# Attention's up product and the output product of a mixer as three fp32r passes over split operands, on one Trainium2 core

## The reference, cut to what matters

```python
y_attn = dsa_branch(q, k, v, qi, ki, wi)                  # 256 x 512
merged = (sigmoid(g_ssm) * (y_ssm @ w_ssm_up)
          + sigmoid(g_attn) * (y_attn @ w_attn_up))       # w_attn_up: 512 x 1024
h = h + merged @ w_out                                    # w_out: 1024 x 1024
hn = rmsnorm(h, norm2_g)
h = h + peer_ffn(hn, peer_wq, ...)                        # starts with hn @ peer_wq
```

## Time and profile before

| what | value |
|---|---|
| median of 3 runs | 2242.0 us (2241.77 to 2243.59) |
| time of the profiled execution | 2244.5 us |
| its span | 2242.8 us, mean granted TensorE clock 0.968 |
| PE busy | 2077.7 us (93%) |
| PEld | 1720.3 us (77%) |
| DVE | 1610.0 us (72%) |
| ACT | 1131.2 us (50%) |
| POOL | 693.7 us (31%) |

### The profile page before, as it was taken

The page is one execution under the profiler, slowest core; times in us unless marked ns, Lnnn a source line. Parts: engine busy times, 40 slices in busy tenths (PEclk is TensorE's granted clock), DMA queues, the critical chain, the costliest instruction groups (busy, mean ns, idle before and its releaser), DMA issues. The chain is left out here.

```text
span 2242.8 us, 33580 instructions
## 1 busy us (share of the span) xinstructions
PE 2077.7 (93%) x11164; PEld 1720.3 (77%) x11164; DVE 1610.0 (72%) x2587; ACT 1131.2 (50%) x1641; POOL 693.7 (31%) x468
## 2 busy tenths in 40 slices
PE   5898999996999889999888999899899999999998
PEld 4775767775877776777676656899899999888887
DVE  4367888887367888888878651399779998555555
ACT  5352767774335376777550233355444444445454
POOL 6620040001757504000030004599967773000000
PEclk8997999998999989999989999999999999999999
DMA  9864789995457658899832333255444445555554
GB/s 394 310 219 148 298 305 354 343 347 193 178 201 294 246 189 322 339 347 343 306 100 75 111 109 146 88 174 174 163 136 145 141 140 180 193 188 191 191 189 150
DMA packets 76634, 485.70 MB, mean 217 GB/s; under 512 B 9472, under 2 KB 9984, under 8 KB 58624
## 3 DMA queue, kind: packets, MB, share of 16 engines
q1 hardware_dynamic: 75824, 482.88, 59.2%
q10 hardware_dynamic: 720, 1.61, 0.2%
HBM read 483.41 MB, written 1.05 MB: 216 GB/s over the span
## 5 line engine op out<-in xcount | busy, mean ns | idle before, releaser
L1191 DVE TENSOR_TENSOR moe_w_lo<-ring,moe_w_hi 128x1024 fp32r<-128x1024 f32 x384 | 467.1, 1252 | 52.1 <-ACT moe_w_hi L1115 38.3
L1115 ACT ACTIVATE moe_w_hi<-ring 128x1024 fp32r<-128x1024 f32 x376 | 385.1, 1058 | 75.0 <-PE bank L1048 43.2
L3083 POOL TENSOR_TENSOR peer_u_lo<-peer_u,peer_u_hi 128x512 fp32r<-128x512 f32 x253 | 343.3, 1368 | 97.0 <-ACT peer_u_hi L3108 95.0
L3023 PE MATMUL bank<-peer_hn_hi,peer_u_hi 128*128 128x256 f32 x1024 | 295.7, 289 | 17.9 <-POOL peer_u_lo L3083 11.9
L3024 PE MATMUL bank<-peer_hn_lo,peer_u_hi 128*128 128x256 f32 x1024 | 287.6, 281 | 0.0
L3025 PE MATMUL bank<-peer_hn_hi,peer_u_lo 128*128 128x256 f32 x1024 | 287.4, 281 | 0.0
L229 POOL TENSOR_TENSOR ret_all_w_lo<-ring,ret_all_w_hi 128x1024 fp32r<-128x1024 f32 x64 | 158.1, 2479 | 293.7 <-ACT ret_all_w_hi L219 293.1
L3108 ACT ACTIVATE peer_u_hi<-peer_u 128x512 fp32r<-128x512 f32 x253 | 159.2, 629 | 129.7 <-PE bank L3025 120.4
L1029 PE MATMUL bank<-moe_w_hi,moe_slots_hi 128*128 128x512 f32 x512 | 210.5, 411 | 11.7 <-DVE moe_w_lo L1191 7.7
L3023 PEld LDWEIGHTS bank<-peer_hn_hi,peer_u_hi 128*128 128x128 f32 x1024 | 194.7, 190 | 19.9 <-POOL peer_u_lo L3083 13.6
L1031 PE MATMUL bank<-moe_w_hi,moe_slots_lo 128*128 128x512 f32 x512 | 201.0, 393 | 0.0
(11 more groups left out here) (517 smaller groups left out, 4570.4 us busy)
## 6 DMA issues: line engine op xcount, KB each, us to landing
ring<-in_stream SPq DMA_DIRECT2D x135, 2048.0 KB, 8.3
peer_u<-in_peer_u SPq DMA_DIRECT2D x128, 512.0 KB, 3.2
peer_scores<-in_peer_v SPq DMA_DIRECT2D x86, 512.0 KB, 4.3
sb_mod_ring<-in_ada_t SPq DMA_DIRECT2D x64, 512.0 KB, 6.4
peer_u<-in_peer_v SPq DMA_DIRECT2D x42, 512.0 KB, 4.3
ret_mod_ring<-in_ada_t SPq DMA_DIRECT2D x32, 512.0 KB, 5.0
s_bz<-in_b_channel SPq DMA_DIRECT2D x4, 512.0 KB, 5.8
ring<-in_stream SPq DMA_DIRECT2D x2, 1024.0 KB, 5.0
```

Of the source, the lines that this page charges most:

```text
L1115: act.activation(w_hi[:, q, :], K.ring[:, at % RING, q * CHUNK // Q:(q + 1) * CHUNK // Q], ACT.Copy).then_inc(hi_done, 1)
L1191: dve.tensor_tensor(w_lo[:, q, :], K.ring[:, at % RING, q * CHUNK // Q:(q + 1) * CHUNK // Q], w_hi[:, q, :].bitcast(F32), ALU.subtract).th ...
L3023: pe.matmul(out, u_hi[:, b, k2, :], h_hi[:, k, :], start=(k == 0), stop=False)
L3083: pool.tensor_tensor(u_lo[:, b, :, :], u[:, i, KD // 2 * half:KD // 2 * (half + 1), :], u_hi[:, b, :, :].bitcast(F32), ALU.subtract).then_ ...
```

## The change

The products of `attn_up` and `project_out` become three fp32r passes each. The 12 quarters of the three weight chunks are rounded on ACT (`split_high`) into rooms that are free then: `queries.w_hi` for attn_up, `queries.w_lo` for n_out, a new `out_w_hi` for n_out+1. GpSimd writes the low parts in place over the ring (`ring_low` is the ring's own memory, read as fp32r). ACT and DVE split the attention output (`attended_high`, `attended_low`) and the merged block (`mixed_hi`, `mixed_low`). A new wait, `act.wait_ge(K.chunk_used, n_out + 1)`, stands ahead of `queries.high`.

```diff
@@ -289,6 +289,8 @@
     sb = lambda n, shape, dt=F32: scope.enter_context(K.nc.sbuf_tensor(n, shape, dt))
     K.hT = sb("hT", [P, KD, T])
     K.mod = sb("mod", [P, 3 * D])
+    with ExitStack() as same_place:
+        K.ring_low = same_place.enter_context(K.nc.sbuf_tensor("ring_low", [P, RING, CHUNK], F32R))
     K.ring = sb("ring", [P, RING, CHUNK])
     K.c_row = sb("c_row", [P, D])
     K.mods, K.mod_bias = sb("mods", [P, 4, MODS]), sb("mod_bias", [P, 4, MODS])
@@ -1935,6 +1937,8 @@
         self.K = K
         NT = S5_TILES
         sb = lambda n, s, scope=scope: scope.enter_context(K.nc.sbuf_tensor(n, s, F32))
+        with ExitStack() as later:
+            self.mixed_hi, self.mixed_lo = (later.enter_context(K.nc.sbuf_tensor(f"mixed_{n}", [P, KD, T], F32R)) for n in ("hi", "lo"))
         self.uT = sb("uT", [P, 4, T])
         self.qT = sb("qT", [P, 4, T])
         self.qiT = sb("qiT", [P, 2, T])
@@ -1957,6 +1961,8 @@
         self.rope = K.c_row[:].rearrange("p (a b t) -> p a b t", a=2, b=2)
     def more_tables(self, scope):
+        with ExitStack() as later:
+            self.high_room = later.enter_context(self.K.nc.sbuf_tensor("out_w_hi", [P, CHUNK], F32R))
         self.last_tables = scope.enter_context(self.K.nc.sbuf_tensor("s5_tables_b", [P, S5_TILES * T], F32))
     def load(self, sp):
@@ -1999,7 +2005,12 @@
         s_(s) for s in ("idx_made", "relu", "score", "score_masked", "pick", "pick_masked"))
     l_made, l_used, max_ready, exp_done, p_ready, p_turned, pT_ready, o_made, o_copied = (
         s_(s) for s in ("l_made", "l_used", "max", "exp", "p", "p_turned", "pT", "o_made", "o_copied"))
-    attn_made, m_ready, m_turned, m_taken = (s_(s) for s in ("attn_made", "m", "m_turned", "m_taken"))
+    attn_made, m_ready, m_turned, m_high, m_low = (s_(s) for s in ("attn_made", "m", "m_turned", "m_high", "m_low"))
+    up_high, up_low, ya_high, ya_low = (s_(s) for s in ("up_high", "up_low", "ya_high", "ya_low"))
+    UP = (n_attn, n_out, n_out + 1)
+    up_rooms = [w[:].rearrange("p q c -> p (q c)") for w in (queries.w_hi, queries.w_lo)] + [S.high_room[:]]
+    quarter = lambda q: slice(q * CHUNK // 4, (q + 1) * CHUNK // 4)
+    ya_halves = [x[:, 0:4, :] for x in (queries.x_hi, queries.x_lo)]
     out_made, x_added, squared, half_ready, std_made, norm_in, hn_ready, hn_turned, hn_high = (
         s_(s) for s in ("out_made", "x_added", "squared", "half_ready", "std", "norm_in", "hn", "hn_turned", "hn_high"))
     hn = K.mod[:, 0:2 * D].rearrange("p (t d) -> p t d", t=TT)
@@ -2069,6 +2080,11 @@
                 pool.wait_ge(pick_ready, tt + 1)
                 pool.affine_select(out=bias[:, tt, own(tt)], in_=bias[:, tt, own(tt)], compare_op=ALU.is_ge, fill=NEG, base=0,
                                    pattern=[[-1, P]], channel_multiplier=1).then_inc(pick_masked, 1)
+            for i, n in enumerate(UP):
+                for q in range(4):
+                    pool.wait_ge(up_high, 4 * i + q + 1)
+                    pool.tensor_tensor(K.ring_low[:, n % RING, quarter(q)], K.ring[:, n % RING, quarter(q)],
+                                       up_rooms[i][:, quarter(q)].bitcast(F32), ALU.subtract).then_inc(up_low, 1)
             queries.low(pool, queries.n0, True)
         @block.tensor
@@ -2278,13 +2294,19 @@
             def attn_up(tt, dh):
-                if tt == 0 and dh == 0:
-                    wait_chunk(pe, K, n_attn)
-                pe.wait_ge(o_copied, 4 * tt + 4)
+                pe.wait_ge(ya_low, tt + 1)
                 pe.wait_ge(pT_ready, len(units))
                 if tt == 1:
                     pe.wait_ge(ssm_taken, 3 + dh)
-                upward(n_attn, S.yaT, tt, dh, 4 + 2 * tt + dh).then_inc(K.chunk_used if tt and dh else attn_made, 1)
+                high, low = (w.rearrange("p (k c) -> p k c", k=4) for w in (up_rooms[0], K.ring_low[:, n_attn % RING, :]))
+                cols, out = slice(dh * 512, (dh + 1) * 512), K.bank[:, 4 + 2 * tt + dh, :]
+                for k in range(4):
+                    pe.wait_ge(up_low, k + 1)
+                    x_high, x_low = (x[:, k, own(tt)] for x in ya_halves)
+                    pe.matmul(out, x_high, high[:, k, cols], start=(k == 0), stop=False)
+                    pe.matmul(out, x_high, low[:, k, cols], start=False, stop=False)
+                    last = pe.matmul(out, x_low, high[:, k, cols], start=False, stop=(k == 3))
+                last.then_inc(K.chunk_used if tt and dh else attn_made, 1)
             def turn_mixed(tt):
                 for half in range(2):
@@ -2296,13 +2318,16 @@
             def project_out(tt, dh):
-                if tt == 0:
-                    wait_chunk(pe, K, n_out + dh)
-                pe.wait_ge(m_taken, 2 * tt + 2)
+                pe.wait_ge(m_low, 2 * tt + 2)
                 pe.wait_ge(l_used if tt else o_copied, len(units))
-                w = K.ring[:, (n_out + dh) % RING, :].rearrange("p (k c) -> p k c", k=KD)
+                high, low = (w.rearrange("p (k c) -> p k c", k=KD) for w in (up_rooms[1 + dh], K.ring_low[:, (n_out + dh) % RING, :]))
+                out = K.bank[:, 2 * tt + dh, :]
                 for k in range(KD):
-                    last = pe.matmul(K.bank[:, 2 * tt + dh, :], K.hT[:, k, own(tt)], w[:, k, :], start=(k == 0), stop=(k == KD - 1))
+                    pe.wait_ge(up_low, 4 * (1 + dh) + (k // 2 + 1))
+                    x_high, x_low = (x[:, k, own(tt)] for x in (S.mixed_hi, S.mixed_lo))
+                    pe.matmul(out, x_high, high[:, k, :], start=(k == 0), stop=False)
+                    pe.matmul(out, x_high, low[:, k, :], start=False, stop=False)
+                    last = pe.matmul(out, x_low, high[:, k, :], start=False, stop=(k == KD - 1))
                 last.then_inc(K.chunk_used if tt == 1 else out_made, 1)
             def turn_normed(tt):
@@ -2449,6 +2474,16 @@
                                K.bank[:, 4 + n % 2, 0:2 * (tt + 1) * P].rearrange("p (m t) -> p m t", t=P),
                                ACT.Copy).then_inc(pT_ready, 1)
+            def split_high(i, q):
+                n = UP[i]
+                if q == 0:
+                    act.wait_ge(K.landed[n % RING], 16 * (n // RING + 1))
+                act.activation(up_rooms[i][:, quarter(q)], K.ring[:, n % RING, quarter(q)], ACT.Copy).then_inc(up_high, 1)
+
+            def attended_high(tt):
+                act.wait_ge(o_copied, 4 * tt + 4)
+                act.activation(ya_halves[0][:, :, own(tt)], S.yaT[:, :, own(tt)], ACT.Copy).then_inc(ya_high, 1)
+
             exponentials(0)
             for n in range(len(units)):
                 if n + 1 < len(units):
@@ -2456,13 +2491,21 @@
                 take_turned(n)
                 if n < TT:
                     take_gate(8 + n, n_last, 3, ACT.Copy)
+                if n >= 4:
+                    for q in (2 * (n % 2), 2 * (n % 2) + 1):
+                        split_high(n // 2 - 2, q)
+                if n == 6:
+                    attended_high(0)
             act.wait_ge(group_taken, 10)
             act.activation(gates[:, 1, :, COLS:D], gates[:, 1, :, COLS:D], ACT.Sigmoid).then_inc(gates_open, 1)
+            attended_high(1)
+            for q in range(4):
+                split_high(2, q)
             for tt in range(TT):
                 for half in range(2):
                     act.wait_ge(m_turned, 2 * tt + half + 1)
-                    act.activation(K.hT[:, 4 * half:4 * half + 4, own(tt)],
-                                   K.bank[:, 4 + 2 * tt + half, :].rearrange("p (k t) -> p k t", k=4), ACT.Copy).then_inc(m_taken, 1)
+                    act.activation(S.mixed_hi[:, 4 * half:4 * half + 4, own(tt)],
+                                   K.bank[:, 4 + 2 * tt + half, :].rearrange("p (k t) -> p k t", k=4), ACT.Copy).then_inc(m_high, 1)
             def square(n):
@@ -2485,6 +2528,7 @@
                 act.activation(queries.x_hi[:, 4 * half:4 * half + 4, own(tt)],
                                K.bank[:, 4 + n, :].rearrange("p (k t) -> p k t", k=4), ACT.Copy).then_inc(hn_high, 1)
+            act.wait_ge(K.chunk_used, n_out + 1)
             queries.high(act, queries.n0, True)
             square(0)
             square(1)
@@ -2695,6 +2739,17 @@
                 dve.tensor_tensor(gates[:, 0, tt, cols], gates[:, 0, tt, cols], K.bank[:, 6 + g % 2, :],
                                   ALU.mult).then_inc(ssm_taken, 1)
+            def attended_low(tt):
+                dve.wait_ge(ya_high, tt + 1)
+                high, low = (x[:, :, own(tt)] for x in ya_halves)
+                dve.tensor_tensor(low, S.yaT[:, :, own(tt)], high.bitcast(F32), ALU.subtract).then_inc(ya_low, 1)
+
+            def mixed_low(n):
+                tt, ks = n // 2, slice(n % 2 * 4, n % 2 * 4 + 4)
+                dve.wait_ge(m_high, n + 1)
+                dve.tensor_tensor(S.mixed_lo[:, ks, own(tt)], K.bank[:, 4 + n, :].rearrange("p (k t) -> p k t", k=4),
```

(10 more changed lines are left out.)

## The result

The change makes the kernel slower by 0.65%: 2258.9 us median (2254.6 to 2260.5, four runs) against 2242.8 us (2241.8 to 2245.1, four runs), ratio 1.0065 (95% interval 1.0054 to 1.0077). Slower was forecast; 2250.0 was not, and 2258.9 lies beyond the range's upper end of 2254.5. A second set of five runs of the same kernel gave 2258.8 us, ratio 1.0062 (1.0048 to 1.0076).

What follows compares the result with a forecast made beforehand. It took TensorE's own work to bound the mixer's end until 1372, then a 6.26 us latency chain. +6.2 to project_out and later delays summed to +8.3, taken as +8: 2252.5 profiled, 2250.0 median, range 2244.5 to 2254.5.

Steps and rivals of the forecast that it cites:

- the sign: Whole kernel: slower, 2250.0 us for the median (+0.36%); chance of slower by over 0.2% put at 0.75.
- the mechanism: Mixer's end: a VectorE instruction with two SBUF operands ends no sooner than 0.54 us after the GpSimd subtraction it meets.
- The late high parts: After project_out(1,0): ACT's peer_wq high parts start only then, take 3.78 us and put square(0) at 1371.2.
- such ones are free: VectorE beside GpSimd: one-operand instructions lose nothing, judged from L2737, which took 0.15 us.
- divide(5): VectorE's divide in unit 5: meets a subtraction, ends at 1319.0, +0.9 us, hidden but for 0.1 behind TensorE.
- the first rival: No mutual blocking; its 3.9 us idle before turn(7) may cost the clock, half speed for 3 us costing 1.5; chance 0.20.
- the forecast's own line: Last turn and attn_up: divide(7) ends at 1332.5, turn(7) is 5.5 us late, attn_up starts about 1335.3 instead of 1329.4.
- +6.2 to project_out: First project_out: starts at 1350.2 against 1344.01, +6.2 us, with TensorE's 2.7 us saving in attn_up inside.
- blocked twice: Sums, lows and divide(7): GpSimd goes first, each may lose another 2.3 us; +12 to +13, 2254.5 us; chance 0.13.
- L1754's worst is 2.61 us, one subtraction: Retention stage's VectorE instruction, at worst 2.61 us, cited against the rival blocked twice.
- No mutual blocking: Mixer's end: VectorE and GpSimd do not block each other; -0.8 us, 2241 to 2244, no change; chance 0.20.
- Faster: the late high parts don't decide: Mixer's end: no blocking, and squares done under project_out; TensorE ends 6.5 us sooner, 2235.5 us; chance 0.05.

Runs made afterwards that it cites:

- e6: Changed kernel with the 128x2 negation of the maxima done as two one-column instructions; ratio 1.0048 to the kernel before, mixer +8.6 us.
- e12: The changed kernel run again without any edit; ratio 1.0062 to the kernel before, mixer +13.9 us.
- e2: Changed kernel with GpSimd's 12 weight subtractions replaced by zero fills, low weight parts left out of the products; ratio 1.0018 to the kernel before, mixer +2.1 us.
- e3: Changed kernel with each GpSimd weight subtraction cut into four pieces of 256 columns; ratio 1.0031 to the kernel before, mixer +4.8 us.
- e10: Changed kernel with zero fills for the weight subtractions and the peer_wq wait moved from ScalarE to GpSimd; ratio 0.9989 to the kernel before, mixer -4.1 us.
- e5: Changed kernel with the peer_wq wait on GpSimd, subtractions in 256-column pieces, and attended_high(0) and attended_low(0) later; ratio 0.9989 to the kernel before, mixer -4.5 us.
- e1: Changed kernel with the wait for the consumed output chunk moved from ScalarE to GpSimd; ratio 1.0034 to the kernel before, mixer +7.3 us.
- e9: e5 plus the one-column negations and peer_wq's first four subtractions in four pieces each; 2239.2 us against 2246.0 before, ratio 0.9983.

## Why the prediction was right or wrong

Right: the sign, the mechanism, and each price for which a row stood. A VectorE instruction with two SBUF operands ends 0.5 us after the subtraction that it meets (0.55 here); three of the four sums take 2.2 us, norm(0) 3.5 (1.42 + 2.3 forecast); mixed_low and add_out are free; TensorE's triples are 0.69 apart (0.678 forecast), and its saving is real: from the first matmul of project_out to the end of its last, with turn_mixed(1) between, 23.3 us (1357.24 to 1380.57) instead of 28.5 (1344.01 to 1372.52). The late high parts: square(0) 21.6 us behind project_out(0,0) where 21.0 was forecast (1371.2 less 1350.2). From project_out's start to the next stage the forecast had +2.1 (8.3 less 6.2), measured +2.6 (37.40 against 34.81).

Wrong: one step, in the paragraph on GpSimd and VectorE, "L2737 at 1357.02, one operand, took 0.15 beside GpSimd: such ones are free", and from it "divide(5) ... ends at 1319.0 (+0.9, hidden but for 0.1 behind TensorE); divide(6) at 1324.3 (+0.6)". L2737 is 128x1. L2716, an instruction of the same kind with 128x2, isn't free: it waits for the subtraction's end (1.32 and 0.87 us instead of 0.17), and then the divide behind it is late for the turn and loses a whole second subtraction. Turns 5 and 6 were 2.3 and 5.1 us late instead of 0.1 and 0.6 (from the mark), the last turn 9.8 instead of 5.5. Then came a smaller one: attn_up was 11.3 late where 5.9 was forecast. TensorE, idle for 6.2 us, did the last turn and values at the lower clock. The windows show length, busy time of each engine and granted clock:

```profile
1334.00:1339.40 5.40, 0.00 (x0) 0.00 (x0) 4.38 (x4) 1.21 (x2) 4.91 (x2) 0.50 0.28 121
1339.50:1343.00 3.50, 3.48 (x17) 3.49 (x18) 0.29 (x1) 2.33 (x3) 0.71 (x1) 0.52 0.00 0
```

From the last turn to attn_up 3.78 us passed instead of 2.34: that 1.4 was priced in the first rival (1.5), and the forecast's own line held 0.4 of it. The later steps gave 0.7 back, project_out being 10.6 late, because it waits for VectorE (its idle time ends with L2750) and not for TensorE's own work. With the negation in one column (e6), the sum came out nearly as worked, +8.6 for +8.3, though attn_up was 1.2 later than forecast there too; the same wait for VectorE covered it. So the term that was mis-sized is "+6.2 to project_out", which measured +10.6, and it was off for a single row's shape.

A small slip changed nothing: the last low part is needed 1.75 calls into project_out, not 1.5; it was ready at 1358.24, before the second call began (1363.68).

The mixer's +13.2 alone would have left the range (2242.0 + 13.2 = 2255.2). The whole miss is 8.9 us (2258.9 for 2250.0): 4.9 in the mixer (13.2 for 8.3), 0.3 from rounding to +8, 0.8 from the median of before (2242.8 with the fourth run, for 2242.0), and 2.9 that the mixer doesn't explain. The stretch ahead of it, which moves by steps of some us between executions, is of that size, but that it makes up the difference of the medians was not shown. In the set of e12 nothing is left over (medians 12.7 us apart, mixer +13.9).

The rival "blocked twice" came nearest in time (+12 to +13). Its mechanism, GpSimd going first when both wait, wasn't at work in the sums, of which three lost one subtraction each. It was in the divides only because the instruction ahead of them, the negation or for divide(7) attended_low(0), had let GpSimd go first; the forecast had that for divide(7). "Against it: L1754's worst is 2.61 us, one subtraction" stayed true: no VectorE instruction of 512 columns took more than 2.73. "No mutual blocking" is ruled out by e2 and e3. "Faster: the late high parts don't decide" names the right second cost: without both, e10 and e5 are 4.1 and 4.5 us faster in the mixer (forecast 6.5). That sum had counted a last turn 2.2 us late for ScalarE's copies (2.1 and 1.5 here). It had not counted that norm(1) meets a subtraction: 2.97 us instead of 1.42 takes 1.5 back.

Row and rule: the negation of 128x2 waited for a subtraction (1.32 us) and for a fill (0.83), that of 128x1 did not (0.15); the sums waited for a subtraction (2.2) and not for a fill (0.69). The Trainium skill (SBUF — State Buffer, section on who interferes with whom) says this: a VectorE instruction with two SBUF inputs contends only with a GpSimd instruction that reads SBUF, while `tensor_scalar`, in a mode that uses both ports, contends with any; and by the Trainium skill (VectorE: DVE Perf Modes, on the mode 2x_2P) that mode needs source and result in SBUF and their outermost non-unit dimension even (or odd and equal in both), which two columns meet, while one column has no such dimension. The waits agree with it; that the mode itself was on, no run here shows. The prediction took only the first half of it, and read the second as its opposite ("The Trainium skill says the same").

## What to carry to other kernels

A pass put on an idle GpSimd isn't free for VectorE: list VectorE's instructions behind each GpSimd one in order and ask of every shape whether it waits, also of the smallest (a tensor_scalar of two columns, both sides in SBUF, waited), because a short instruction that waits decides who goes next. Cut the GpSimd instructions short, and the same work costs little more than a third in the mixer (e3: +4.8 for +13.2), for some 20% more of GpSimd's time. Keep two-operand SBUF instructions of VectorE off the critical path. When a room is borrowed, put the wait for it on the engine that has nothing queued behind it (e1: 5.8 us for one line).

## What the runs showed of the hardware

- A VectorE tensor_scalar of 128x2 fp32, SBUF to SBUF, waited for GpSimd's subtraction (0.86 to 2.37 us instead of 0.17) and for its fill (0.83), and ended within 0.03 us of it, while 128x1 ran beside a subtraction in 0.14 to 0.15. Reciprocals of 128x2 took 0.15 beside a running subtraction (e6). A two-operand divide ended 0.55 us after the subtraction. That two elements a partition decide over 4.6 us was the surprise.
- When VectorE waits right behind a running subtraction, it goes ahead of the next one (e6: 1.08 and 1.53 us); when it comes a moment later, it loses a whole one more (2.73).
- A GpSimd subtraction of 128x1024 took 2.4 us, and four of them in a row that met nothing started 2.3 us apart (9.28 for four, in the kernel before). In pieces of 256 columns each took 0.73 and started 0.69 apart (e9), 2.8 us for the same elements.
- After the same idle time of 2.2 us TensorE went on at a granted clock of 1.00 in one execution of the changed kernel and of 0.51 in the other (e12); after 6.2 us it was at 0.52.
